# Values of three MLA head pairs in matmuls of 384 columns, with the late pieces in a new order

## The reference

```python
def mla_attention(cq, ckv, k_rope_raw, q_norm, kv_norm, w_uq, w_ukv, pos):
    q = (rms_norm(cq, q_norm) @ w_uq).reshape(B, S, H, dq).transpose(0, 2, 1, 3)
    q = jnp.concatenate([q[..., :MLA_NOPE], rope(q[..., MLA_NOPE:], pos)], axis=-1)
    kv = (rms_norm(ckv, kv_norm) @ w_ukv).reshape(B, S, H, MLA_NOPE + MLA_V).transpose(0, 2, 1, 3)
    k_nope, v = kv[..., :MLA_NOPE], kv[..., MLA_NOPE:]
    ...
        s = jnp.einsum('bhqd,bhkd->bhqk', qb, k) * scale
        p = masked_softmax(s, tq[:, None] >= pos[None, :])
        return jnp.einsum('bhqk,bhkd->bhqd', p, v)
```

## Time and profile before

| | us |
|---|---|
| median of 3 runs | 1527.79 (1527.57 to 1528.78) |
| span of the profiled execution | 1525.5 |
| TensorE busy | 1502.5 (98%) |
| VectorE busy | 886.8 (58%) |
| ScalarE busy | 718.2 (47%) |
| GpSimd busy | 437.7 (29%) |

### The profile page before, as it was taken

How to read it: one execution, slowest core, us unless ns; L and a number is a source line. 1 busy time by engine, 2 the same in 40 slices (tenths; PEclk the granted TensorE clock), 3 DMA queues, 4 the chain that set the end, 5 groups by cost and what they waited for, 6 DMA issues and landing times.

```text
span 1525.5 us, 21251 instructions
## 1 busy us (share of the span) xinstructions
PE 1502.5 (98%) x7396; PEld 1257.8 (82%) x7396; DVE 886.8 (58%) x1531; ACT 718.2 (47%) x1308; POOL 437.7 (29%) x459
## 2 busy tenths in 40 slices
PE   8999999999999999999999999999999999999998
PEld 6888888887888888888888888888878888888886
DVE  6874866767553544535557666667575535354454
ACT  6863777874422222222367547878643212222222
POOL 1302677774020100101022036767720101010011
PEclk9999999999999999999999999999999999999999
DMA  6343221135323333333323422212333333332233
GB/s 210 98 153 121 79 84 63 43 98 174 102 93 100 94 100 95 98 95 96 98 83 125 172 67 80 76 63 63 116 127 97 97 97 97 96 96 96 96 96 111
DMA packets 43362, 154.29 MB, mean 101 GB/s; under 512 B 5440, under 2 KB 5440, under 8 KB 43280
## 3 DMA queue, kind: packets, MB, share of 16 engines
q1 hardware_dynamic: 37296, 133.77, 27.8%
q0 software_dynamic: 5696, 18.94, 3.5%
q10 hardware_dynamic: 288, 0.52, 0.1%
HBM read 142.73 MB, written 10.49 MB: 100 GB/s over the span
## 4 chain that ended last, share of the span: by engine, by line
PE 86%; DVE 4%; ACT 4%; issue 3%; DMA 1%; POOL 1%; POOLq 0%; DVEq 0%; SPq 0%; ACTq 0%
PE G L1472 14%; PE G L1474 13%; PE G L1473 13%; PE O L1474 9%; PE O L1473 9%; PE O L1472 9%; PE O L1762 3%; PE T L1738 3%; PE S L1713 2%; PE T L1472 2%; PE T L1473 2%; PE T L1474 2%; ACT F L667 1%; PE O L1547 1%; DVE F L1413 1%
## 5 line engine op out<-in xcount | busy, mean ns | idle before, releaser
L615 ACT ACTIVATE wsplit<-stage 128x1024 fp32r<-128x1024 f32 x227 | 240.2, 1058 | 602.4 <-PE G L1474 272.6
L976 DVE TENSOR_TENSOR wsplit<-stage,wsplit 128x1024 fp32r<-128x1024 f32 x180 | 262.4, 1458 | 72.9 <-ACT wsplit L615 72.7
L601 POOL TENSOR_TENSOR F<-Y 128x512 f32<-128x512 f32 x64 | 68.5, 1070 | 637.3 <-DVE Y L1430 637.3
L1472 PE MATMUL G<-xg,wsplit 128*128 128x512 f32 x576 | 231.7, 402 | 7.3 <-DVE wsplit L1002 6.9
L1473 PE MATMUL G<-xg,wsplit 128*128 128x512 f32 x576 | 225.6, 392 | 0.0
L1474 PE MATMUL G<-xg,wsplit 128*128 128x512 f32 x576 | 225.5, 391 | 0.0
L1208 DVE CUSTOM_DVE_ANT_0 F<-S,F 128x512 f32<-128x512 f32 x192 | 93.5, 487 | 98.8 <-PE S L1713 67.5
L499 POOL TENSOR_TENSOR wsplit<-stage,wsplit 128x1024 fp32r<-128x1024 f32 x46 | 111.3, 2419 | 124.4 <-ACT wsplit L615 124.2
L786 ACT ACTIVATE F<-F,nmx 128x512 f32<-128x512 f32 x192 | 107.7, 561 | 63.4 <-DVE nmx L1208 61.8
L1472 PEld LDWEIGHTS G<-xg,wsplit 128*128 128x128 f32 x576 | 108.8, 189 | 29.3 <-DVE wsplit L1002 6.9
L1474 PEld LDWEIGHTS G<-xg,wsplit 128*128 128x128 f32 x576 | 108.6, 189 | 24.0
(11 more groups left out here) (292 smaller groups left out, 3023.3 us busy)
## 6 DMA issues: line engine op xcount, KB each, us to landing
stage<-units SPq DMA_DIRECT2D x229, 512.0 KB, 3.5
stage_n<-units_n SPq DMA_DIRECT2D x20, 512.0 KB, 4.0
gates<-Y POOLq DMA_DIRECT2D x32, 256.0 KB, 2.8
E<-gates POOLq DMA_DIRECT2D x24, 256.0 KB, 3.5
F<-gates POOLq DMA_DIRECT2D x8, 256.0 KB, 4.0
x<-x_in SPq DMA_DIRECT2D x3, 512.0 KB, 6.9
rope<-tables POOLq DMA_DIRECT2D x1, 768.0 KB, 6.0
out<-F SPq DMA_DIRECT2D x3, 256.0 KB, 2.3
```

The source lines that it names most:

```text
L601: pool.tensor_tensor(F[:, m % 2, :], Y[:, m % 2, :], Y[:, m % 2, :], ALU.mult)\
L615: act.activation(wslot(u)[:, 0, :], staged(u), ACT.Copy).then_inc(s_whin if u in SN else s_whi, 1)
L976: dve.tensor_tensor(wslot(u)[:, 1, :], staged(u), wslot(u)[:, 0, :], ALU.subtract)\
L1472: pe.matmul(dst, a(0), b(0), start=first, stop=False)
```

## The change

The values of pairs 1, 2 and 3 are made together: for each of the four token tiles one product with 384 columns of weights (three pairs), three matmuls, in a tile of its own (`("MV", 1, tt)`, tt 0 to 3). The weights for it stand in the unit of MLA 1, columns 640 to 1024; the units of MLA 2 and 3 end with the key product. The pieces of MLA 1 are therefore seven (two queries, keys, four of values), those of MLA 2 and 3 three each. Each pair's values have a place: `pcT[:, 0]`, the two halves of the area behind 8192, and `pcT[:, 1]`. ScalarE and VectorE empty a values' tile with two instructions each (pairs 1 and 2 together, pair 3). The table of steps is changed to fit, and with it `SPLIT_STEP` (worked out from it): WA 0 is split at step 77 instead of 73 and first used at 78 instead of 76; MLA 3 is split at 78 instead of 79 and first used at 82 instead of 81; WA 1 is split at 82 and used at 85 (81 and 84 before). From step 90 on every piece stays at its step. The semaphore that counted the products (`s_mready`) now counts ten a layer, and one more (`s_mvals`) counts the first three values' tiles.

```diff
--- before.py
+++ after.py
@@ -95,8 +95,8 @@
 for n in range(len(DURING) * PIECES):
     at = FIRST_STEPS[n] if n < 3 * PIECES else 11 + (n - 3 * PIECES) * 4 // 3
     FILL[at].append((DURING[n // PIECES], n % PIECES))
-for item, steps in ((("MLA", 1), (65, 66, 67, 71)), (("MLA", 2), (73, 74, 75, 78)), (("WA", 0), (76, 77, 79, 80)),
-                    (("MLA", 3), (81, 82, 83, 86)), (("WA", 1), (84, 85, 87, 88)), (("WA", 2), (90, 91, 93, 94)),
+for item, steps in ((("MLA", 1), (65, 66, 67, 71, 72, 74, 76)), (("MLA", 2), (73, 75, 77)), (("WA", 0), (78, 79, 80, 81)),
+                    (("MLA", 3), (82, 83, 84)), (("WA", 1), (85, 86, 87, 88)), (("WA", 2), (90, 91, 93, 94)),
                     (("WA", 3), (96, 97, 98, 99))):
     for piece, i in enumerate(steps):
         FILL[i].append((item, piece))
...
@@ -118,7 +118,7 @@
 
     name, i = item
     if name == "MLA":
-        return [("MQ", i, 0), ("MQ", i, 1), ("MK", i, 0), ("MV", i, 0)][piece]
+        return [("MQ", i, 0), ("MQ", i, 1), ("MK", i, 0)][piece] if piece < 3 else ("MV", i, piece - 3)
     if name == "WA":
         return ("A", 2 * i + piece // 2)
     return item
...
@@ -166,7 +166,9 @@
 
 
 QK_AFTER = [NSA_NJ // 2, NSA_NJ, NSA_NJ + 8, NSA_NJ + 16]
-V_AFTER = [8, NSA_NJ // QT, NSA_NJ // QT + 2, NSA_NJ // QT + 4]
+V_AFTER = [8, NSA_NJ // QT]
+MREADY = {(p, piece): (3 * p if p < 2 else 2 * p + 2) + piece + 1 for p in range(PAIRS) for piece in range(3 if p < 2 else 2)}
+NMREADY = len(MREADY)
 MHI, MLO = {}, {}
 for i in range(STEPS):
     for t in EMPTY_AT[i] + EMPTY_AT[i - 1]:
...
@@ -259,7 +261,10 @@
         MQ = area[:, 0:4096].rearrange("p (s e c n) -> p s e c n", s=2, e=2, c=2)
         MK = area[:, 4096:8192].rearrange("p (s e c n) -> p s e c n", s=2, e=2, c=2)
         MV = [pcT[:, 0, :, :].rearrange("p c n -> p (c n)").rearrange("p (t e n) -> p t e n", t=QT, e=2),
-              area[:, 8192:9216].rearrange("p (t e n) -> p t e n", t=QT, e=2)]
+              area[:, 8192:9216].rearrange("p (t e n) -> p t e n", t=QT, e=2),
+              area[:, 9216:10240].rearrange("p (t e n) -> p t e n", t=QT, e=2),
+              pcT[:, 1, :, :].rearrange("p c n -> p (c n)").rearrange("p (t e n) -> p t e n", t=QT, e=2)]
+        MV12 = area[:, 8192:10240].rearrange("p (a t e n) -> p t a e n", a=2, t=QT, e=2)
         H = area[:, 0:8192].rearrange("p (c m n) -> p c m n", c=2, m=KT)
         PT = area_b[:, :].rearrange("p (s c n) -> p s c n", s=2, c=2)
         TB = area_b[:, 0:4096].rearrange("p (k j c n) -> p k j c n", k=2, j=16, c=2)
...
@@ -811,17 +817,27 @@
                     act.activation(MQ[:, p % 2, e, 0, :], E[:, e, :], ACT.Copy).then_inc(s_mhi, 1)
 
                 def mla_k(p):
-                    act.wait_ge(s_mready, l * 12 + (3 * p + 3))
+                    if p < 2:
+                        act.wait_ge(s_mready, l * NMREADY + MREADY[p, 2])
+                    else:
+                        act.wait_ge(s_wused, l * NU + (UNIT["MLA", p] + 1 + WUSED0))
                     for e in range(2):
                         ins = act.activation(MK[0:64, p % 2, e, 0, :], g_tile(("MK", p, 0))[64 * e:64 * e + 64, :], ACT.Copy)
                     ins.then_inc(s_mhi, 1)
 
-                def mla_v(p):
+                def mla_v(p, tt):
                     act.wait_ge(s_pv, l * NHP + V_AFTER[p])
-                    act.wait_ge(s_wused, l * NU + (UNIT["MLA", p] + 1 + WUSED0))
-                    src = g_tile(("MV", p, 0))[:, :].rearrange("p (a n) -> p a n", n=HD)
-                    act.activation(MV[p % 2][:, :, :, 0:HD].rearrange("p t e n -> p (t e) n"), src, ACT.Copy)\
-                        .then_inc(s_mhi, 1)
+                    if p == 1 and tt < QT - 1:
+                        act.wait_ge(s_mvals, l * (QT - 1) + (tt + 1))
+                    else:
+                        act.wait_ge(s_wused, l * NU + (UNIT["MLA", p] + 1 + WUSED0))
+                    if p == 0:
+                        src = g_tile(("MV", 0, 0))[:, :].rearrange("p (a n) -> p a n", n=HD)
+                        act.activation(MV[0][:, :, :, 0:HD].rearrange("p t e n -> p (t e) n"), src, ACT.Copy).then_inc(s_mhi, 1)
+                    else:
+                        src = g_tile(("MV", 1, tt))[:, 0:384].rearrange("p (a e n) -> p a e n", e=2, n=HD)
+                        act.activation(MV12[:, tt, :, :, 0:HD], src[:, 0:2], ACT.Copy)
+                        act.activation(MV[3][:, tt, :, 0:HD], src[:, 2], ACT.Copy).then_inc(s_mhi, 1)
 
                 act.wait_ge(s_init, 2)
                 if l == 0:
...
@@ -1231,7 +1247,7 @@
                 def mla_rotate(p, e):
                     if p > 0:
                         dve.wait_ge(s_mlo, l * NMLO + (MLO["MQ", p - 1, e] + 1))
-                    dve.wait_ge(s_mready, l * 12 + (3 * p + e + 1))
+                    dve.wait_ge(s_mready, l * NMREADY + MREADY[p, e])
                     dve.tensor_tensor(E[:, e, :], g_tile(("MQ", p, e))[:, :], tabM, ALU.mult).then_inc(s_gfree, 1)
 
                 def gated_half(m):
...
@@ -1258,11 +1274,17 @@
                                                 MK[0:64, p % 2, e, 0, :], ALU.subtract)
                     ins.then_inc(s_gfree, 1)
 
-                def mla_v(p):
-                    dve.wait_ge(s_mhi, l * NMHI + (MHI["MV", p, 0] + 1))
-                    src = g_tile(("MV", p, 0))[:, :].rearrange("p (a n) -> p a n", n=HD)
-                    both = MV[p % 2][:, :, :, :].rearrange("p t e n -> p (t e) n")
-                    dve.tensor_tensor(both[:, :, HD:P], src, both[:, :, 0:HD], ALU.subtract).then_inc(s_gfree, 1)
+                def mla_v(p, tt):
+                    dve.wait_ge(s_mhi, l * NMHI + (MHI["MV", p, tt] + 1))
+                    if p == 0:
+                        src = g_tile(("MV", 0, 0))[:, :].rearrange("p (a n) -> p a n", n=HD)
+                        both = MV[0][:, :, :, :].rearrange("p t e n -> p (t e) n")
+                        dve.tensor_tensor(both[:, :, HD:P], src, both[:, :, 0:HD], ALU.subtract).then_inc(s_gfree, 1)
+                    else:
+                        src = g_tile(("MV", 1, tt))[:, 0:384].rearrange("p (a e n) -> p a e n", e=2, n=HD)
+                        dve.tensor_tensor(MV12[:, tt, :, :, HD:P], src[:, 0:2], MV12[:, tt, :, :, 0:HD], ALU.subtract)
+                        dve.tensor_tensor(MV[3][:, tt, :, HD:P], src[:, 2], MV[3][:, tt, :, 0:HD], ALU.subtract)\
+                            .then_inc(s_gfree, 1)
 
                 def merged_lo(m):
                     dve.wait_ge(s_mghi, l * KT + (m + 1))
...
@@ -1645,7 +1667,11 @@
                             ins = three(dst[:, :], wtile(u, 2 * k + piece), rows(cn, k), k == 0, k == 1)
                         ins.then_inc(s_mready, 1)
                     elif piece == 2:
-                        three(dst[:, :], wtile(u, 4), rows(cn, 2), True, True).then_inc(s_mready, 1)
+                        three(dst[:, :], wtile(u, 4), rows(cn, 2), True, True).then_inc(s_mready if p < 2 else s_wused, 1)
+                    elif p == 1:
+                        tt = piece - 3
+                        three(dst[:, 0:384], lambda c: cn[:, c, 2, tt * P:(tt + 1) * P], lambda c: wslot(u)[:, c, 640:1024],
+                              True, True).then_inc(s_mvals if tt < QT - 1 else s_wused, 1)
                     else:
                         for tt in range(QT):
                             ins = three(dst[:, tt * P:(tt + 1) * P], lambda c: cn[:, c, 2, tt * P:(tt + 1) * P],
...
@@ -1749,15 +1775,15 @@
                         emptied(("WT", 1))
                     if opens and n >= 2:
                         pe.wait_ge(s_ofree, l * NHEAD + (n - 1))
-                    if opens and not nsa and e == 0:
-                        emptied(("MV", t, 0))
+                    if opens and not nsa and e == 0 and t < 2:
+                        emptied(("MV", t, 0 if t == 0 else QT - 1))
                     if nsa and br == 1 and kt == 0:
                         gr, b = t // 2, 2 * (t % 2) + e
                         emptied(("WT", gr))
                         for c in range(2):
                             pe.matmul(dst[:, :], vblk[:, gr, b, :], pcT[:, gr, c, :], start=False, stop=False,
                                       skip_group_check=True)
-                    v = VN[:, kt, br, t // 2, :] if nsa else MV[t % 2][:, kt, e, :]
+                    v = VN[:, kt, br, t // 2, :] if nsa else MV[t][:, kt, e, :]
                     for c in range(2):
                         ins = pe.matmul(dst[:, kt * P:S], v, PT[:, slot, c, kt * S:(kt + 1) * S - kt * P],
                                         start=opens and c == 0, stop=closes(j) is not None and c == 1,
...
@@ -1955,7 +1981,9 @@
         for p in range(PAIRS):
             head = np.concatenate([r(96), r(80, 96), r(64, 80)])
             uq = _columns(w["mla_w_uq"][l], np.concatenate([192 * p + head, 192 * p + 96 + head]))
-            kv = [256 * p + 128 * e + o + r(64) for o in (0, 64) for e in range(2)]
```

(6 more changed lines are left out.)

## The result

The changed kernel takes 1538.78 us (median of 5 runs, 1538.59 to 1539.33) against 1527.79, 11.0 us more; over all executions of both the ratio is 1.0069, with a 95% interval of 1.0058 to 1.0081. That lies in the range on record and on the side that was forecast, but 4.4 us from the forecast of 1534.4. It is the time of a rival: "The clock falls ... 1539", which had 12%.

What follows compares the result with a forecast made beforehand. TensorE, busy 1502.5 of 1525.5 us, was taken to bound the kernel. Per layer -1.8 - 0.9 + 1.4 + 4.6 = +3.3 us, so 1527.8 + 6.6 = 1534.4 us; range 1529.8 to 1539.

Steps and rivals of the forecast that it cites:

- The clock falls: Rival: TensorE's long wait drops its clock to half for 4 to 5 us once per layer, giving 1539 us; 12%.
- What is removed: Values of pairs 1 to 3: twelve 384-column matmuls replace 36 of 128, 0.55 us a group, saving 1.8 us per layer.
- the wait at MLA 3: At step 81, TensorE's wait for MLA 3's split weights goes, saving 0.9 us per layer.
- The bank: At step 73, the second query product waits for the first values' tile to be emptied: 1.4 us added per layer.
- The weights of WA 0: At step 78, TensorE wants WA 0 at 295.7 but its split weights are ready at 300.3: 4.6 us wait per layer.
- The sum: All terms together: +3.3 us per layer, +6.6 over both layers, giving 1534.4 us.
- what was costed at nothing: Extra evacuations, work queued behind the waits, WA 1's split and SP's loads: taken as 0, bound 1 us a layer.

Runs made afterwards that it cites:

- run 6: Changed kernel with both parts of WA 0's split moved ahead, values made in 128-column matmuls instead of 384: 1528.9 us, ratio 1.0009.
- run 5: Changed kernel with ScalarE's high part of WA 0's split at the head of step 77 and GpSimd's rest moved into step 76: 1528.8 us, ratio 1.0000.
- run 2: Changed kernel with only ScalarE's high part of WA 0's split moved to the head of step 77: 1538.1 us, ratio 1.0053.
- run 1: Changed kernel with twelve unused 512-column matmuls filling TensorE's wait for WA 0's weights at step 78: 1532.7 us, ratio 1.0024.
- run 3: Kernel before, all matmuls 128 columns, only the step table changed so MLA 1's last piece is at 76 and WA 0 starts at 78: 1555.2 us.
- run 4: Changed kernel with ScalarE's high part of WA 0's split ahead and its rest made by VectorE at step 77 instead of GpSimd: 1534.1 us, ratio 1.0028.
- run 12: Kernel before with the table of run 3, but MLA 3 at steps 82 to 85 and WA 1 at 86 to 89: 1542.9 us, ratio 1.0091.
- run 7: As run 5, with the first values' tile emptied sooner by ScalarE and VectorE: 1528.5 us, ratio 1.0000.
- run 8: Changed kernel with another step table: MLA 1's last values at 75, WA 0 and all behind it one step later: 1529.4 us, ratio 1.0005.
- run 11: As run 10, plus the first values' tile emptied sooner and twelve unused matmuls a layer in the wait of step 70: 1525.4 us, ratio 0.9977.
- run 9: As run 7, plus twelve unused 128-column matmuls a layer in TensorE's wait of step 70: 1526.9 us, ratio 0.9986.
- run 10: Changed kernel with only the table changed: MLA 1's last values at 75, MLA 2 at 73, 76, 77, WA 0 from 79: 1527.05 us, ratio 0.9988.

## Why the prediction came out as it did

*What is removed.* Right. 0.57 us a group for 0.55, the wait at MLA 3 gone (step 81 is 1.0 and 1.1 us shorter). By the 56 ns that the Trainium skill (TensorE: Matmul & The Clock Gate, "Wait — 56ns, not 53.3ns?") gives for 128 columns, run 6 would have been no different from run 5, as an estimate. The trace does not agree: its step 71 was 0.47 us longer.

*The bank.* Right: 1.18 us for 1.4, released by VectorE's values.

*The weights of WA 0.* Right in place and size: 4.12 us for 4.6, since the weights came at 300.43 for 300.3 and TensorE at 296.3 for 295.7; the maximum of step 77 stood at 294.97 for 294.9:

```profile
294.97 0.54 DVE L1224 CUSTOM_DVE_ANT_0 F<-S,F 128x384 f32<-128x384 f32 x1
```

The working beneath was incomplete: it took GpSimd to be free when ScalarE was done, and GpSimd was free 0.25 us later (run 2). For the changed kernel's time that makes no difference; for a cure it does, since the wait only gives way when both queues are moved (runs 2 and 5).

*The sum.* Without the clock the terms give +3.3 a layer; run 1 shows +2.7. That part, 5.5 us for 6.6, is the mechanism forecast; the shorter wait for WA 0 is 0.5 us a layer of the difference.

*The step that failed.* "The clock falls: this would be the longest wait within the kernel's work; the longest of these now is 1.5 us, without a loss of clock ... 12%." No row of before told what a wait of 4 us does, and I let that count for a clock that holds. Run 1 shows the fall and its price, 4.2 us, where the rival had 4.6; runs 2, 3, 4 and 12 show falls of the clock again, behind waits from 2.6 us on. Sized by the start it was right, and it should have been the likeliest case.

*What was not foreseen at all.* The tail, 1.4 us: among what was costed at nothing, no term was for the instruction stream. 5.5 + 4.2 + 1.4 = 11.1 us, and 11.0 were measured. That this is the clock rival's 1539 to 0.2 us, and that it lies just inside the range, is in part luck: 1.1 us too much for the waits and 0.4 too much for the clock were made up by a tail that no case had.

*Open.* Which queue's fetch it is (TensorE's, by the count of matmuls) was not tried. That the packet holds the gate's DMA up is argued from their coming together in seven kernels of seven and in none of the others; why a packet of 16 KB should cost 0.7 to 1.8 us is not shown. Nor was what sets how long the clock stays low.

## What to carry to other kernels

When a piece is moved that holds a double-buffered slot, count the steps between the slot's release and its next use, and follow every queue in between: here two steps fewer cost 4 us twice, and a table with the release one step sooner and the use one step later brought them back. A wait of 4 us on TensorE was paid twice here, once idle and once at half the clock behind it; weigh that as the likely case as soon as the wait is longer than any that the trace shows to be harmless. And a saving on TensorE counts only as far as the next wait: of 1.9 us a layer saved by wide matmuls 0.5 was left (runs 5 and 6).

## What the runs showed of the hardware

The clock does not fall at one length of wait. It held behind 1.5 us in the profiled execution of the kernel before and behind 1.56 in run 5, and fell behind 2.6 in run 4. In runs 3 and 12 steps 71 and 72 had no piece at all; there it held three times behind the old 1.5 us of step 70 and fell once, in layer 0 of run 12:

```profile
282.00:286.00 4.00, 4.00 (x16) 3.62 (x16) 2.40 (x7) 3.78 (x10) 3.44 (x6) 0.60 0.00 0
```

That the same wait of 4.1 us cost 2.7 us of clock in one layer and 1.45 in the other (6.8 and 3.4 us at the low level in the changed kernel, and the other way round in run 2) shows that the length of the wait alone does not set the price. It also fell without a long wait: in the profiled executions of runs 6, 7, 8 and 11, 9 to 10 us before the end of the span, for 3.4 us each time, with no idle time of TensorE over 0.2 us in the 10 us before; there its dense matmuls of 512 columns give way to short ones, of 1 and 128 columns. In run 7:

```profile
1517.70:1521.20 3.50, 3.50 (x19) 3.50 (x18) 1.97 (x3) 1.88 (x3) 1.14 (x2) 0.51 0.59 221
```

A single profiled execution can therefore differ from the next by half a microsecond or more for this reason alone.

Where a 16 KB packet of instructions falls into a burst of gate loads, the 256 KB transfers of run 7 land 1.3 us later at the median than in run 9, where it comes 4.2 us before the burst; 12 matmuls a layer decide which.

VectorE's operations on two tiles in SBUF and GpSimd's operations slow each other (2.20 us for 1.23 and 2.08 for 1.26 in run 4), and the delay has a fixed end: a sum of 128x512 that takes 0.69 us alone ends 0.5 us behind GpSimd's split of 2.4 us, whether it starts 0.3 or 1.4 us into it (2.65 and 1.55 us, runs 10 and 7).
